# First mixer of a two-layer encoder: the rotation's swap of head halves by transfers instead of a matmul, weight splits moved ahead of the turned tiles, and the first two score tiles moved inside the second value block

## What is computed

```python
def apply_rope(x, cos, sin):
    x1, x2 = x[..., :half], x[..., half:]
    return jnp.concatenate([x1 * c - x2 * s, x1 * s + x2 * c], axis=-1)

def even_mixer(h, ...):
    qa, ka, va, qb, kb, vb = split_cols(h @ w_in, [512, 512, 512, 512, 512, 512])
    qa = apply_rope(qa, cos, sin); ka = apply_rope(ka, cos, sin)
    oa = diff_attention(qa, ka, va, lam, subln_g, lam_init)   # softmax(q k) twice per head, difference, times v
    ob = neighbourhood_attention(qb, kb, vb, rpb)
    return concatenate([oa, ob]) @ w_out

for l in range(2):
    x = x + 0.5 * swiglu(rmsnorm(x)); x = x + mixer(rmsnorm(x)); x = x + 0.5 * swiglu(rmsnorm(x))
```

## Time and profile before

| | us |
|---|---|
| median of 3 runs (lowest to highest) | 1924.08 (1922.45 to 1928.21) |
| the profiled execution, its own time | 1926.7 |
| its span, first to last instruction | 1924.9 |
| PE busy in it | 1886.9 (98%) |
| DVE, ACT, POOL busy | 1303.0, 922.7, 222.4 |
| the stretch of the change, start of block 2 to the first score tile of the loop | 372.96 to 440.22 |

### The profile page before, as it was taken

How to read it: one execution, slowest core, us unless ns; L and a number is a source line. 1 busy time by engine, 2 the same in 40 slices (tenths; PEclk the granted TensorE clock), 3 DMA queues, 4 the chain that set the end, 5 groups by cost and what they waited for, 6 DMA issues and landing times.

```text
span 1924.9 us, 31514 instructions
## 1 busy us (share of the span) xinstructions
PE 1886.9 (98%) x11366; PEld 1645.8 (85%) x11366; DVE 1303.0 (68%) x1913; ACT 922.7 (48%) x1590; POOL 222.4 (12%) x200
## 2 busy tenths in 40 slices
PE   8999999999999999999999999999999999999998
PEld 7899988787888889998888999888776788999886
DVE  6898842667556679983357999435785677898423
ACT  5455522437556445553243555324477543555323
POOL 0100000210233210000021000002146221000001
PEclk9999999999989999999999999999999999999999
DMA  5223322222211323333222332322311022333321
GB/s 179 69 107 109 123 98 106 81 88 56 89 44 45 102 73 110 108 110 110 90 84 88 105 114 92 127 92 86 118 66 45 23 77 77 111 108 109 124 95 44
DMA packets 36574, 177.20 MB, mean 92 GB/s; under 512 B 12544, under 2 KB 14080, under 8 KB 16016
## 3 DMA queue, kind: packets, MB, share of 16 engines
q1 hardware_dynamic: 34496, 173.24, 26.4%
q10 hardware_dynamic: 1808, 2.32, 0.4%
q0 software_dynamic: 192, 0.59, 0.1%
HBM read 174.04 MB, written 2.10 MB: 92 GB/s over the span
## 4 chain that ended last, share of the span: by engine, by line
PE 91%; DVE 3%; ACT 2%; POOL 1%; DMA 1%; issue 1%; ACTq 0%; POOLq 0%; DVEq 0%
PE ps L358 29%; PE ps L360 28%; PE ps L359 28%; PE ps L1632 1%; DVE wl L286 1%; PE ps L1655 1%; PE ps L1162 1%; ACT wh L282 1%; PE ps L1234 1%; DMA raw<-in_units 1%; POOL xg L2471 1%; PE ps L1361 0%; PE ps L1224 0%; PE ps L1144 0%; DVE xgl L411 0%
## 5 line engine op out<-in xcount | busy, mean ns | idle before, releaser
L358 PE MATMUL ps<-xgh,wh 128*128 128x256 f32 (+1 forms) x1504 | 511.3, 340 | 10.1 <-DVE xgl L707 3.9
L360 PE MATMUL ps<-xgh,wl 128*128 128x256 f32 (+1 forms) x1504 | 504.4, 335 | 0.0
L359 PE MATMUL ps<-xgl,wh 128*128 128x256 f32 (+1 forms) x1504 | 503.4, 335 | 0.0
L286 DVE TENSOR_TENSOR wl<-raw,wh 128x2048 fp32r<-128x2048 f32 (+1 forms) x92 | 213.8, 2324 | 351.6 <-ACT wh L282 351.4
L358 PE MATMUL ps<-tmh,wh 128*128 128x256 f32 (+1 forms) x1344 | 411.3, 306 | 0.0
L359 PE MATMUL ps<-tml,wh 128*128 128x256 f32 (+1 forms) x1344 | 410.5, 305 | 0.0
L360 PE MATMUL ps<-tmh,wl 128*128 128x256 f32 (+1 forms) x1344 | 410.1, 305 | 0.0
L282 ACT ACTIVATE wh<-raw 128x2048 fp32r<-128x2048 f32 (+1 forms) x92 | 174.6, 1898 | 359.4 <-PE ps L360 358.1
L358 PEld LDWEIGHTS ps<-xgh,wh 128*128 128x128 f32 x1504 | 284.6, 189 | 45.4 <-issue 7.2
L359 PEld LDWEIGHTS ps<-xgl,wh 128*128 128x128 f32 x1504 | 284.7, 189 | 29.6 <-issue 2.2
L360 PEld LDWEIGHTS ps<-xgh,wl 128*128 128x128 f32 x1504 | 284.6, 189 | 29.2
(11 more groups left out here) (312 smaller groups left out, 2595.4 us busy)
## 6 DMA issues: line engine op xcount, KB each, us to landing
raw<-in_units SPq DMA_DIRECT2D x160, 1024.0 KB, 4.9
out<-xg SPq DMA_DIRECT2D x4, 512.0 KB, 4.0
relb<-in_rpb SPq DMA_DIRECT2D x64, 24.0 KB, 2.1
x<-in_xT ACTq DMA_DIRECT2D x2, 512.0 KB, 6.8
x<-in_xT SPq DMA_DIRECT2D x2, 512.0 KB, 7.6
raw<-in_units SPq DMA_DIRECT2D x2, 256.0 KB, 5.5
raw<-in_units ACTq DMA_DIRECT2D x2, 256.0 KB, 9.5
cosA<-in_rope_a ACTq DMA_DIRECT2D x1, 256.0 KB, 2.6
```

The lines of the kernel that those rows point to most:

```text
L286: nc.vector.tensor_tensor(wl[:, c % 2, 0:n], raw[:, c % 2, 0:n], wh[:, c % 2, 0:n].bitcast(F32), ALU.subtract).then_inc(w_lo, 1)
L358: nc.tensor.matmul(dst, lh, rh, start=first, stop=False, skip_group_check=onto)
L359: nc.tensor.matmul(dst, lh, rl, start=False, stop=False, skip_group_check=onto)
L360: return nc.tensor.matmul(dst, ll, rh, start=False, stop=last, skip_group_check=onto)
```

## The change

`rot_pe` and the matrix `permA` go. In their place ACT issues four DMAs per block (`rot_act`), each of 32 partitions by 512 floats (64 KB), from `q32` to a new tile `rq`: partition groups 0 and 1, and 2 and 3, trade places. The sign goes into the sines' table on the host. `rq` has two slots with one semaphore each. On ACT and DVE the split of the next unit moves from the head of an even round to the inside of an odd round, behind `rot_act(i)` and `q32(i)` and ahead of the rest of block i - 1's rotation; it is the split of unit c + 2 in the new count, which is the same unit as before. The first two score tiles move from between the value blocks to behind the second tile of v = 1, with their exponentials on ACT; DVE splits unit BE + 6 ahead of their maxima.

```diff
-        permA = sb("permA", [P, P], F32, diff_mem)
+        rq = sb("rq", [P, 2, SEQ], F32, diff_mem)
-        def rot_pe(pe, i):
-            pe.wait_ge(q32_done, i + 1)
+        def rot_act(act, i):
+            act.wait_ge(q32_done, i + 1)
             if i >= 2:
-                pe.wait_ge(qs_done, i - 1)
-            nc.tensor.matmul(ps[:, 2 + i % 2, :], permA[:, :], q32[:, i % 2, :],
-                             start=True, stop=True).then_inc(rot_done, 1)
+                act.wait_ge(qs_done, i - 1)
+            for r in range(0, P, 32):
+                o = r ^ 32
+                act.dma_start(rq[r:r + 32, i % 2, :], q32[o:o + 32, i % 2, :]).then_inc(rot_in[i % 2], 16)
@@ even_load: three tables instead of four before the first wait
-            for dst, src in ((cosA, ...), (sinA, ...), (permA, perm_d[:, 0:P])):
+            for dst, src in ((cosA, ...), (sinA, ...)):
@@ even_pe
                 if i == 3:
                     norm_reads_pe(pe)
-                rot_pe(pe, i - 2)
-            rot_pe(pe, 6)
...
-                    if v == 0 and t == 0:
-                        rot_pe(pe, 7)
-                if v == 0:
-                    pe.wait_ge(qa_lo, 8)
-                    diff_scores_pe(pe, 0)
-                    diff_scores_pe(pe, 1)
+                    if v == 1 and t == 1:
+                        pe.wait_ge(qa_lo, 8)
+                        diff_scores_pe(pe, 0)
+                        diff_scores_pe(pe, 1)
@@ even_act
-                if i % 2 == 0:
-                    split_hi(act, c + 1)
                 if i == 0:
+                    split_hi(act, BE + 1)
                     norm_act(act, 1, 4)
...
+                rot_act(act, i)
+                if i % 2:
+                    split_hi(act, c + 2)
                 if i >= 1:
                     qa_hi_act(act, i - 1)
-            split_hi(act, BE + 5)
             qa_hi_act(act, 7)
@@ even_dve
-                if i % 2 == 0:
-                    split_lo(dve, c + 1)
...
                 nc.vector.tensor_tensor(q32[:, i % 2, :], ps[:, qa_bank(i), :], rB[:, :], ALU.mult).then_inc(q32_done, 1)
+                if i % 2:
+                    split_lo(dve, c + 2)
                 if i >= 1:
                     qa_dve(dve, i - 1)
...
-            split_lo(dve, BE + 5)
             qa_dve(dve, 7)
+            split_lo(dve, BE + 6)
+            diff_max_dve(dve, 0)
+            diff_max_dve(dve, 1)
@@ qa_dve
-            dve.wait_ge(rot_done, i + 1)
+            dve.wait_ge(rot_in[i % 2], 64 * (i // 2 + 1))
-            nc.vector.tensor_tensor(qs[:, i % 2, :], ps[:, 2 + i % 2, :], sinA[:, :], ALU.mult).then_inc(qs_done, 1)
+            nc.vector.tensor_tensor(qs[:, i % 2, :], rq[:, i % 2, :], sinA[:, :], ALU.mult).then_inc(qs_done, 1)
```

More of the change, by code:

```diff
@@ L979, in build_trunk @@
         qc_done = sem("qc_done")
-        rot_done = sem("rot_done")
+        rot_in = [sem("rot_in0"), sem("rot_in1")]
         qs_done = sem("qs_done")
@@ L1789, in even_load @@
             act.wait_ge(x_new, 8)
-            for dst, src in ((cosA, rope_a[0:P, :]), (sinA, rope_a[P:2 * P, :]), (permA, perm_d[:, 0:P])):
+            for dst, src in ((cosA, rope_a[0:P, :]), (sinA, rope_a[P:2 * P, :])):
                 act.dma_start(dst[:, :], src).then_inc(even_in, 16)
@@ L1807, in even_pe @@
             norm_pe(pe, 1, 4)
-            pe.wait_ge(even_in, 64)
+            pe.wait_ge(even_in, 48)
             for i in range(2, 8):
@@ L1853, in even_act @@
                 c = BE + i // 2
-                if i % 2 == 0:
-                    split_hi(act, c + 1)
                 if i == 0:
+                    split_hi(act, BE + 1)
                     norm_act(act, 1, 4)
-                    act.wait_ge(even_in, 64)
+                    act.wait_ge(even_in, 48)
                 if i == 1:
@@ L1874, in even_act @@
                                          scale=col(C_RN + t)).then_inc(va_done, 1)
-                if v == 0:
-                    diff_exp_act(act, 0)
-                    diff_exp_act(act, 1)
+                    if v == 1 and t == 1:
+                        diff_exp_act(act, 0)
+                        diff_exp_act(act, 1)
             diff_act(act)
@@ L1931, in even_dve @@
         def even_dve(dve):
-            dve.wait_ge(even_in, 64)
+            dve.wait_ge(even_in, 48)
             nc.vector.tensor_tensor(lamp, lamb.rearrange("p (a b e) -> p a b e", a=2, b=2)[:, :, 0, :],
@@ L1939, in even_dve @@
                 c = BE + i // 2
-                if i % 2 == 0:
-                    split_lo(dve, c + 1)
                 if i == 0:
+                    split_lo(dve, BE + 1)
                     norm_dve(dve, 1)
@@ L1959, in even_dve @@
                     nc.vector.tensor_copy(col(C_RN, 4), ps[:, 5, 0:4]).then_inc(rcol_read, 1)
-            split_lo(dve, BE + 5)
             qa_dve(dve, 7)
[L1962 to L1974, removed]
+            split_lo(dve, BE + 6)
+            diff_max_dve(dve, 0)
+            diff_max_dve(dve, 1)
+            dve.wait_ge(lam_done, 4)
+            diff_rec_dve(dve, 0)
+            diff_comb_dve(dve, 0)
             diff_dve(dve)
@@ L2061, in even_pool @@
         def even_pool(pool):
-            pool.wait_ge(even_in, 64)
+            pool.wait_ge(even_in, 48)
             for i in range(8):
@@ L2683 @@
     perm = np.concatenate([rope_perm(64, P, 0), rope_perm(32, P, 0)], axis=1)
+    turn_sign = np.ones((2 * P, 1), np.float32)
+    turn_sign[P:][np.arange(P) % 64 < 32] = -1.0
     arrays = {
@@ L2686 @@
         "consts": small, "colvec": colvec, "lamvec": i["diff_lam"][0].reshape(-1), "rpb": rpb.reshape(-1),
[L2687 removed]
+        "ident": np.eye(P, dtype=np.float32), "perm": perm, "rope_a": rope_rows(64, P, 0) * turn_sign,
         "rope_d": rope_rows(32, P, 0), "masks": window_masks(),
```

1 line of the change is left out of this document (removed).

## The result

| | before | after |
|---|---|---|
| median of 7 runs each | 1924.05 us (1922.02 to 1928.21) | 1934.87 us (1933.47 to 1941.12) |
| profiled execution, its span | 1926.7, 1924.9 | 1934.87, 1932.4 |
| first score tile of the loop | 440.22 | 451.97 |

The ratio is 1.0056, 95% interval 1.0045 to 1.0068: 0.56% slower, 10.8 us. The forecast was 5.5 us slower, 1929.6, and the range ended at 1934.5, so the time lies outside it. Slower by over 0.3% had been given 0.43.

What follows compares the result with a forecast made beforehand. PE, busy 98%, was taken to bound the kernel, with the chain DVE - ACT - DVE nearly as slow. A loop 3.8 us later plus 1.7 of clock loss made 5.5 us on 1924.1: 1929.6 us, range 1925.0 to 1934.5.

Steps and rivals of the forecast that it cites:

- D: On ACT's queue, time from the first of a block's four issues to ACT's next instruction: taken as 1.75 us.
- The prediction's own chain: DVE - ACT - DVE path through rotations, issues and splits: 11.6 + D per pair of rounds, loop at 435.3 + 5D.
- The five groups: Groups of four issues on the path before the loop; each 0.1 us of D costs 0.5 us.
- while D stays under 2.0: Even rounds: issues hidden, since the sum to be rounded is ready some 2.0 us after q32.
- may pay this too, but once: DVE's qs, reading two operands beside POOL's product, may slow as the add did, 1.19 instead of 0.69 us.
- The 2.70 of the bias table: Upper end for D, from 64 starts at 0.68 us each; at that price the time is 1936.5 us.
- The clock: PE after the stall ahead of v = 1: 3.4 us at half speed, 1.7 us lost.
- The stalls: PE's waits: 2.3 us at BE + 3, 2.2 at BE + 4, 7.0 ahead of v = 1.
- The landing: Arrival of swapped blocks before DVE's qs: hidden, costed at nothing; at 8 us it would cost 1 to 4.
- Slower than can be missed: Rival: larger D or longer clock fall, slower by over 0.3%; 1930.5 us at D = 1.91, 1936.5 at 2.70; chance 0.43.
- Issues are nearly free: Rival: D near 0 on ACT, chain 4.9 us earlier less 1.7 for the clock, 1920.9 us; chance 0.06.
- The change does what it takes away: Rival: only PE counts, 7.6 us gained from products and a wait, 1916.5 us; chance 0.03.

Runs made afterwards that it cites:

- e3_one_issue: Changed kernel with one issue of 128 partitions per block instead of four of 32, head halves not swapped: 1926.40 us, ratio 1.0016 to the kernel before.
- e1_order_only: Kernel before with only the splits moved behind the odd block's q32 on ACT and DVE, swap still on PE: 1923.66 us, ratio 0.9989.
- e5b_wide_rows: Changed kernel with four issues per block of 128 partitions by 128 floats from q32, swap left out: 1937.56 us, one run.
- e5_hbm_source: Changed kernel with the same four issues reading a table in HBM, swap left out: 1934.0 us, one run.
- e7_busy_stall: Changed kernel with 46 filler matmuls on PE in the stall ahead of v = 1: 1933.89 us, one run.
- e4_pool_issue: Changed kernel with the four transfers of a block issued from POOL's queue, ahead of its cosine product: 1926.09 us, ratio 1.0001 to the kernel before.
- e14_pool_copies: Changed kernel with splits ahead of issues, first value copies and DVE's maxima earlier, and issues from POOL: 1917.41 us, ratio 0.9958 to the kernel before.
- e12_split_first: Changed kernel with ACT's split ahead of the four issues in odd rounds, same queue: 1925.31 us, ratio 0.9998 to the kernel before.
- e8_scores_only: Kernel before with only the first two score tiles moved, exponentials and maxima with them: 1926.70 us, ratio 1.0008.
- e2_swap_only: Kernel before with only the swap by ACT's transfers, splits and score tiles where they were: 1930.75 us, ratio 1.0030.
- e6_copies_early: Changed kernel with ACT's copies of the first value block ahead of the last rounding: 1933.86 us, ratio 1.0039 to the kernel before.
- e13_first_copies: Changed kernel with splits ahead of issues, first value copies before block 6's rounding, DVE's maxima before its split: 1921.36 us, ratio 0.9966 to the kernel before.

## Why the prediction was wrong

**The step that failed is D**, "I take D = 1.75". It measured 2.54. The prediction's own chain, with the measured D put in for the assumed one, against the trace:

| step | by the prediction's chain | with D = 2.54 | measured | rest |
|---|---|---|---|---|
| block 4 (BE + 2) | 381.7 + 2D | 386.8 | 386.90 | 0.1 |
| block 6 (BE + 3) | 393.3 + 3D | 400.9 | 401.68 | 0.8 |
| v = 0 (BE + 4) | 404.9 + 4D | 415.1 | 417.11 | 2.0 |
| v = 1 | 422.0 + 5D | 434.7 | 437.16 | 2.5 |
| loop | 435.3 + 5D + clock | 449.6 | 451.97 | 2.4 |

(In the last line 1.6 stand for the clock.) The five groups account for 5 x 0.79 = 4.0 us of the miss at the loop. The rest of 2.4 has two causes. The path from qs to the next q32 in an even round takes 3.98, 4.44 and 3.95 us instead of 3.28, 2.5 in all, and e3_one_issue parts the two: with one issue instead of four it is 3.70, 3.69 and 3.69.

- The difference to e3, 0.28, 0.75 and 0.26, is 1.3 us. It follows from D: the prediction hid the issues of even rounds "while D stays under 2.0", and groups of 2.5 to 3.0 us are not hidden. It had this term, at 2.1 us, but only at its far end of D.
- What e3 keeps, 0.4 three times, is 1.2 us and does not follow from D. POOL's product takes 1.67 us instead of 1.27 beside a qs step that reads `rq` (in e1_order_only, where qs reads a PSUM bank, it keeps 1.27 to 1.29), and the add ends 0.55 behind the product. The prediction said of qs that it "may pay this too, but once" and put nothing into its sum; and it read the add's 1.19 in the earlier trace rows as a slower step, where it is a wait for the product.

The sum then stands: 435.3 + 12.7 + 2.5 + 1.5 = 452.0, measured 451.97, with the clock's 1.5 as the distance from v = 1 to the loop, 14.8, less the 13.3 of the earlier trace rows.

**Where the choice went wrong.** Three rows were at hand: 0.48 per issue on the same queue, 0.333 and 0.68 on SP. The prediction corrected the first one downwards, because the transfers are narrower. e5b_wide_rows shows that width does nothing, and e5_hbm_source that the difference unweighed, the source in the core's own memory, costs 0.17 us each. The trace of before had a row with such a source, and the prediction did not use it: at its end SP issues four DMAs in a row from `xg`, in the core's own memory, to HBM.

```profile
L2518 SPq DMA_DIRECT2D out<-xg x4: 353/606/1187, 1918.0 to 1919.6; - x4
```

Its median of 0.606 us, though of another queue and of 512 KB each, is that of the change, 0.612; four are 2.42, and by the prediction's own sum 5 x 2.42 - 4.9 + 1.7 = 8.9, that is 1933.0. The 2.70 of the bias table was named as an end, and the range then stopped at D = 2.3; up to its own price at 2.70, 1936.5, it would have held the time.

**The clock** was right in its loss: the stretch behind the stall shows it, in the windows (us, PE, PEld, DVE, ACT, POOL busy, granted clock, DMA share, GB/s):

```profile
386.00:392.00 6.00, 5.10 (x12) 4.04 (x13) 5.10 (x7) 0.63 (x1) 1.66 (x1) 0.50 0.57 187
...
417.00:423.00 6.00, 5.89 (x27) 5.89 (x28) 4.84 (x7) 0.63 (x1) 1.66 (x1) 0.50 0.58 197
...
437.00:444.40 7.40, 7.24 (x48) 7.16 (x48) 2.67 (x2) 2.91 (x5) 0.00 (x0) 0.78 0.15 25
444.40:452.00 7.60, 7.60 (x63) 6.92 (x62) 3.50 (x5) 3.63 (x10) 0.00 (x0) 1.00 0.50 161
```

0.78 over 7.4 us is 7.4 x 0.22 / 0.5 = 3.3 us at 1.2 GHz, 1.6 lost; 1.7 was forecast, and e7_busy_stall gives 1.4 back. The two falls at 386 and 417 cost PE more, some 2.6 us each, but the kernel nothing, as forecast, since a stall is left behind each (1.02 and 5.62): without the falls those would be longer. What the Trainium skill ("TensorE: Matmul & The Clock Gate", What's actually happening) says, that activity releases the higher clock, the fillers bear out.

**The stalls.** At v = 1 7.0 were forecast and 5.6 came; 4.2 instead of 2.2 at v = 0, 1.0 instead of 2.3 at block 6. One of 2.49 ahead of block 4 was not named: the prediction let PE begin block 4 at 385.3, though PE is free for it at 384.4 (386.90 less 2.49), and 381.7 + 2D passes 384.4 from D = 1.35 on. Block 6's stall is short because PE came late to it, at 400.66 instead of 396.3: 1.6 by the later start of block 4, and 2.8 since its two blocks took 13.76 us instead of 11.0, at a granted clock of 0.80. In the same way v = 0 took 14.4 us at 0.79, which shortened the stall ahead of v = 1. Where PE waits changes with D; that the chain DVE - ACT - DVE sets the end, and by how much for each 0.1 us, held.

**The landing** was costed at nothing, and nothing it is: 2.0 us, and no step waits for it in the change. With the issues on POOL, where the splits are earlier, two steps do, 2.0 us together (e4_pool_issue).

**A reading of the rows.** The prediction has the score tiles at 426.91 "wait for the end of that chain". PE did not wait there: its row has no idle time, and the last value tile's matmul before it begins at 426.70. The chain ended in time, some 0.3 us ahead. The conclusion, to cost the chain beside PE, holds all the same.

**The rivals.** "Slower than can be missed" came true by its own mechanism; its price at D = 2.54 is 5 x 2.54 - 4.9 + 2.5 + 1.5 = 11.8. "Issues are nearly free" falls with 0.612 us each on ACT. The Trainium skill ("DMA: Bandwidth & Descriptors", Issuing engines are not separate DMA queues) has the sequencer's issue time as usually small relative to the DMA itself. Here an issue takes 0.612 us beside 2.0 to landing, and the four of a block, which follow each other, 2.44: for this kernel the measurement speaks against it. "The change does what it takes away" was wrong for the change; e14_pool_copies, with three further moves, gets near it: 1917.41 against the 1916.5 of that rival.

**From the stretch to the time.** The score tile is 11.75 us later, the median 10.8, the two profiled spans only 7.5. That last gap is in another stage. The shift is 11.8 at the stall that ends at 559.54 before and 571.34 after, and 7.5 at the same matmul some 50 us further on:

```profile
609.75 0.47 PE L358 MATMUL ps<-xgh,wh 128*128 128x512 f32 x1 [0.33 <-DVE x L1451]
617.24 0.47 PE L358 MATMUL ps<-xgh,wh 128*128 128x512 f32 x1 [0.33 <-DVE x L1452]
```

In between the earlier trace rows have 0.50 behind the stall that ends at 559.54; in the changed kernel's profile the same stall, 2.56 us, ends near 571.3. The windows of before, then of after:

```profile
552.00:582.00 30.00, 27.45 (x149) 23.42 (x148) 16.94 (x50) 19.40 (x47) 14.90 (x21) 0.83 0.00 1
```

```profile
560.00:590.00 30.00, 27.45 (x169) 23.18 (x168) 18.18 (x55) 19.37 (x48) 15.47 (x21) 1.00 0.01 4
```

0.83 over 30 us is 30 x 0.17 / 0.5 = 10.2 us at half speed, which cost 5.1 at the most, and 4.3 by the two shifts; after lost none. The profiled run of before is itself 2.7 us above its median. So the stretch's own shift is to be read at the score tile, and the medians bear it out.

## What to carry to other kernels

Before DMA issues are put on a computing engine's queue, count them: each takes its time from that engine, here 0.61 us with a source in the core's own memory, and what counts is what stands behind them in program order, not the bytes. With 20 of its 32 issues ahead of splits on which two engines wait, this change came out 11.75 us behind the old kernel at the loop's start, and with all but the first four behind the splits 1.2 us (e12_split_first). When a path is relieved on the busiest engine, look for the next chain in the trace and move its steps first: the copies that release PE's banks, moved together with two maxima, were worth 7.1 us here, as much as the removed products. And look for the row that is nearest in kind, in the whole trace: the issue with a source in the core's own memory stood at the trace's end.

## What the runs showed of the hardware

- An issue from POOL takes 0.498 us, from ACT 0.612 (both from the core's own memory), from ACT with a source in HBM 0.443.
- A step of DVE that reads two operands from the core's memory ends some 0.56 us behind a POOL product that runs at the time, as if it began only then. In e4_pool_issue qs (2.06 instead of 0.69) ends at 394.95 and the product at 394.39; beside the next product the low part of the rounding, which does not need the product at all, takes 2.09 and ends at 402.13, that product at 401.56. It goes the other way too: in the change, beside a qs step that started 0.16 us earlier, the product takes 1.67 instead of 1.27. Which step is held depends on when POOL's product starts, and so an issue moved to POOL moves the hold.
- After one and the same stall of some 2.5 us near 559, with nothing changed there, the granted clock differs from run to run: no fall in the profiled runs of after, e3_one_issue and e4_pool_issue, 3.4 us at half speed in e8_scores_only, e5b_wide_rows, e12_split_first, e7_busy_stall and e14_pool_copies, 6.8 in e1_order_only, and 10.2 in before, e2_swap_only, e5_hbm_source, e6_copies_early and e13_first_copies. The runs of the kernel before fit this: those under 1922.6 us have a mean granted clock of 0.995 to 0.996, those over 1928.2 one of 0.991 to 0.993. By an estimate from these, 0.0035 of 1925 us is 6.7 us, which is their distance. The clock then accounts for the spread; in which stage it falls in which run stays open.
